# Layer norm rows applied one stage later, and each mixer's first products placed in the layer end before it

## The reference

```python
mod = cond @ ada_w[i] + ada_b[i]            # shift, scale, gate for two sites
h = x * (1 + scale[0]) + shift[0]
y = mixer_i(h)                              # 0 mlstm, 1 windowed attention, 2 hgrn2, 3 differential attention
x = layer_norm(ALPHA * x + (1 + gate[0]) * y, ln_g[i, 0], ln_b[i, 0])
h = x * (1 + scale[1]) + shift[1]
y = (silu(h @ w_gate) * (h @ w_up)) @ w_down
x = layer_norm(ALPHA * x + (1 + gate[1]) * y, ln_g[i, 1], ln_b[i, 1])
```

## Time and profile before

| | |
|---|---|
| time, median of 3 runs | 2500.95 us (2500.87 to 2510.68) |
| the profiled execution | 2511.77 us, of which the span is 2510.0 us |
| PE busy | 2339.4 us, 93% |
| DVE busy | 1841.5 us, 73% |
| ACT busy | 1165.9 us, 46% |
| POOL busy | 129.1 us, 5% |
| DMA | 575.95 MB, mean 229 GB/s |

### The profile page before, as it was taken

The page is one execution under the profiler, slowest core; times in us unless marked ns, Lnnn a source line. Parts: engine busy times, 40 slices in busy tenths (PEclk is TensorE's granted clock), DMA queues, the critical chain, the costliest instruction groups (busy, mean ns, idle before and its releaser), DMA issues. The chain is left out here.

```text
span 2510.0 us, 34924 instructions
## 1 busy us (share of the span) xinstructions
PE 2339.4 (93%) x14183; PEld 2064.0 (82%) x14183; DVE 1841.5 (73%) x2124; ACT 1165.9 (46%) x1260; POOL 129.1 (5%) x229
## 2 busy tenths in 40 slices
PE   7999988999999999899999988999997999998997
PEld 7888667788787888687998877898886998887996
DVE  6887676588888888666887637886585887676545
ACT  4342333477677777443443432443642443453442
POOL 1000100000000000001110000110001110000000
PEclk9999989899999999999999989999998999998999
DMA  8843642599999999566898225994534898334551
GB/s 302 255 136 101 198 151 68 161 360 366 357 365 360 358 366 354 198 215 212 268 371 293 93 101 162 369 345 124 167 107 145 281 369 290 97 126 148 187 186 68
DMA packets 414099, 575.95 MB, mean 229 GB/s; under 512 B 68848, under 2 KB 313072, under 8 KB 413936
## 3 DMA queue, kind: packets, MB, share of 16 engines
q1 hardware_dynamic: 393200, 498.17, 59.9%
q0 software_dynamic: 20736, 75.51, 8.0%
HBM read 572.54 MB, written 1.05 MB: 229 GB/s over the span
## 5 line engine op out<-in xcount | busy, mean ns | idle before, releaser
L286 DVE TENSOR_TENSOR st_lo<-st_raw,st_hi 128x2048 fp32r<-128x2048 f32 (+1 forms) x194 | 441.1, 2281 | 220.3 <-ACT st_hi L276 219.9
L276 ACT CAST st_hi<-st_raw 128x2048 fp32r<-128x2048 f32 (+1 forms) x194 | 367.4, 1899 | 358.9 <-PE ps L316 307.4
L314 PE MATMUL ps<-sb_h_hi,st_hi 128*128 128x256 f32 x1608 | 457.2, 284 | 15.5 <-DVE sb_h_lo L961 6.9
L315 PE MATMUL ps<-sb_h_lo,st_hi 128*128 128x256 f32 x1608 | 456.4, 284 | 0.0
L316 PE MATMUL ps<-sb_h_hi,st_lo 128*128 128x256 f32 x1608 | 456.3, 284 | 0.0
L286 DVE TENSOR_TENSOR es_lo<-es_raw,es_hi 128x2048 fp32r<-128x2048 f32 x192 | 428.1, 2285 | 1.1 <-ACT es_hi L276 0.8
L276 ACT CAST es_hi<-es_raw 128x2048 fp32r<-128x2048 f32 x192 | 367.6, 1915 | 85.7 <-PE ps L316 61.8
L314 PEld LDWEIGHTS ps<-sb_h_hi,st_hi 128*128 128x128 f32 x1608 | 309.0, 192 | 19.4 <-issue 10.1
L315 PEld LDWEIGHTS ps<-sb_h_lo,st_hi 128*128 128x128 f32 x1608 | 309.2, 192 | 1.6
L316 PEld LDWEIGHTS ps<-sb_h_hi,st_lo 128*128 128x128 f32 x1608 | 309.2, 192 | 0.2
L314 PE MATMUL ps<-st_hi,sb_h_hi 128*128 128x256 f32 (+1 forms) x528 | 186.2, 353 | 28.0 <-DVE st_lo L286 22.4
(11 more groups left out here) (680 smaller groups left out, 4211.0 us busy)
## 6 DMA issues: line engine op xcount, KB each, us to landing
st_raw<-in_ffn_w_in_dram SPq DMA_DIRECT2D x88, 1024.0 KB, 7.4
t_aw<-in_ada_w_dram POOLq DMA_DIRECT2D x144, 512.0 KB, 7.1
es_raw<-in_w_expert_gate_dram SPq DMA_DIRECT2D x128, 512.0 KB, 6.5
es_raw<-in_w_expert_up_dram SPq DMA_DIRECT2D x128, 512.0 KB, 8.1
es_raw<-in_w_expert_down_dram SPq DMA_DIRECT2D x64, 1024.0 KB, 7.3
st_raw<-in_ffn_w_out_dram SPq DMA_DIRECT2D x44, 1024.0 KB, 7.0
fb_aw<-in_ada_w_dram SPq DMA_DIRECT2D x39, 512.0 KB, 6.1
hs_raw<-in_w_in_dram SPq DMA_DIRECT2D x36, 512.0 KB, 7.9
```

The source lines that it names most:

```text
L276: act.copy(p.at(self.hi[:, m % self.held, :]), p.at(self.raw[:, n % self.slots, :])).then_inc(self.high, 1)
L286: dve.tensor_tensor(p.at(self.lo[:, m % self.held, :]), p.at(self.raw[:, n % self.slots, :]), p.at(self.hi[:, m % self.held, :]).bitcast(F ...
L314: pe.matmul(out, a_hi, b_hi, start=start, stop=False, skip_group_check=True)
L315: pe.matmul(out, a_hi, b_lo, start=False, stop=False, skip_group_check=True)
```

## The change

1. **Old rows in the mixer.** A class `PastNorm` loads the two rows of layer `i - 1`'s last norm at the start of mixer `i` (for mixers 1 to 3), and DVE applies them there: at marks 16 and 26 in the windowed and the differential mixer, after pieces 2 and 3 of the first projection in `hgrn`. The tail neither loads nor applies them. It also loads only the two `lnr` rows that it uses (four in the last layer).
2. **First products in the layer end.** At the end of tails 0 to 2 the 13 dummy matmuls go, and PE does the first piece of the next mixer (48 matmuls of 256 columns) as the splits come: `open_tokens` ahead of the windowed and differential mixer, `open_features` ahead of `hgrn`. ACT and DVE also lift and lower the next mixer's second piece in the layer end. The mixer skips what is taken.
3. **Finer first splits.** `divide` goes in five steps (blocks 0, 1, 2-3, 4-5, 6-7), at both sites; one transposed block moves to another PSUM bank.
4. **Initial stage.** DVE lowers the first weight piece ahead of its splits of the normed input; PE does that piece (24 matmuls) in this stage; ACT and DVE lift and lower two more there.
5. **Last norm.** For the last layer each token block is done by two fused instructions for each half (subtract the mean and multiply by gain; multiply by the spread's root and add the bias), the first block before the second one's adds.

```diff
@@ layer_tail, SP
+            S.send(sp, f0 + 2)
+            lines = [A["ln_g_2"][layer, 0], A["ln_b_2"][layer, 0]]
+            if final:
+                lines += [A["ln_g_2"][layer, 1], A["ln_b_2"][layer, 1]]
-            if layer:
-                for r, v in enumerate((A["ln_g_2"][layer - 1, 1], A["ln_b_2"][layer - 1, 1])):
-                    sp.dma_start(past[:, r, :], rows(v)).then_inc(past_landed, 16)
...
-            S.send(sp, S.reach(f_end, min(f_end + 1, len(S.pieces))))
+            S.send(sp, S.reach(f_end, min(f_end + 2, len(S.pieces))))
@@ layer_tail, PE
                 turn_norm(1, 1)
-                stir(k, pe, 0, 13)
+                ready = lambda kt: (hs, len(SPLITS) + splits_for(kt))
+                (open_features if layer == 1 else open_tokens)(k, pe, ready)
@@ layer_tail, ACT
             if not final:
+                S.lift(act, f_end + 2)
                 act.wait_ge(merged, 1)
                 modulated(1)
@@ layer_tail, DVE
-            if layer:
-                scale_past(0)
             S.lower(dve, o + 4)
-            if layer:
-                scale_past(1)
...
+            def centre_row(t):
+                for c in range(2):
+                    cols = slice(c * BANK, (c + 1) * BANK)
+                    dve.scalar_tensor_tensor(X[:, t, cols], X[:, t, cols], mv[:, 1, t, 0:1], lnr[:, 2, cols],
+                                             ALU.subtract, ALU.mult).then_inc(centred, 1)
...
             if not final:
+                normalise(1, 1)
                 divide(1)
+                S.lower(dve, f_end + 2)
@@ new
+class PastNorm:
+    def load(self, sp):
+        for r, name in enumerate(("ln_g_2", "ln_b_2")):
+            sp.dma_start(self.rows[:, r, :], rows(self.A[name][self.layer - 1, 1])).then_inc(self.landed, 16)
+    def scale(self, dve, t):
+        x = self.k.X[:, t, :]
+        dve.wait_ge(self.landed, 32)
+        dve.tensor_tensor(x, x, self.rows[:, 0, :], ALU.mult).then_inc(self.step, 1)
+        dve.wait_ge(self.step, t + 1)
+        dve.tensor_tensor(x, x, self.rows[:, 1, :], ALU.add).then_inc(self.done, 1)
+
+def open_tokens(k, pe, ready):
+    S = k.stream
+    wh, wl = S.take(pe)
+    for kt in range(8):
+        pe.wait_ge(*ready(kt))
+        for t in range(2):
+            last = product(pe, k.ps[:, 0, t * HB:(t + 1) * HB], k.h_hi[:, kt, t * P:(t + 1) * P],
+                           k.h_lo[:, kt, t * P:(t + 1) * P], wh[:, kt, :], wl[:, kt, :], kt == t == 0, kt == 7)
+    last.then_inc(S.used, 1)
@@ windowed, DVE
-            weave(w.dve_chunks(dve), masks_in(dve), w.dve_ropes(dve, cos, sin), w.dve_biases(dve), w.dve_mixes(dve),
-                  w.dve_stores(dve))
+            weave(w.dve_chunks(dve), masks_in(dve), w.dve_ropes(dve, cos, sin), past.scaling(dve, (16, 26)),
+                  w.dve_biases(dve), w.dve_mixes(dve), w.dve_stores(dve))
```

117 lines of the change are left out of this document (79 added, 38 removed).

## The result

The changed kernel took 2478.58 us (median of 10 runs, 2468.70 to 2505.52), the kernel before 2505.40 us (10 runs, 2500.32 to 2512.06): 0.9904 of it, 95% interval 0.9875 to 0.9934. That is faster, as forecast, but by 26.8 us and not by 40.3, and outside the range of 2450 to 2475. The two profiled executions hide this: 2510.0 us of span before, 2469.0 after, a difference of 41.0 us.

The account below looks back on a forecast made before the run. TensorE, busy almost everywhere, was taken to be bound by waits for VectorE's lower halves of weight pieces and at layer boundaries. 28.3 + 3.7 + 2.0 + 1.5 + 2.5 + 3.3 - 1.0 = 40.3 us off 2500.95 gave 2460.7, range 2450 to 2475.

Parts of the forecast that it names:

- Step 1: Tails of layers 1 to 3: moving the old norm's rows out gains 28.3 us, lower bound 22.4.
- Step 2: Mixers 1 to 3: applying the old rows on VectorE there costs 1 us in all, bounds 0 and 5.
- Step 3: Layer ends 0 to 2: early first products gain 3.7 us ahead of `hgrn`, 2.0 windowed, 1.5 differential.
- the new boundary is 2.1 us later than the old: Layer ends: lowering the second piece there delays the next mixer's start by 2.1 us; the 48 products finish under it.
- the clock rival: Layer ends and woven mixers: 48 products at low clock lose 3.5 us per end, new waits 1.5; 2474 us, chance 14%.
- 3.7 us gained: Layer 1's end into `hgrn`: 5.8 us of warm products leave the mixer, less 2.1 for the later boundary.
- TensorE waits 2.7 us: Start of the windowed mixer: new TensorE wait for the first rotation, leaving a gain of 2.0 us, bounds 0.5 and 5.
- three small instructions more in the same place: Differential mixer's start: no copies but three small instructions more at the first rotation; gain 1.5 us, bounds 0.5 and 5.
- Step 4: Finer first splits, first site: gain 0, at most 0.7 us in each of four layers; wait after G0 about 1 us.
- Step 5: Initial stage: TensorE's first product comes earlier, near 14.2 us; gain 2.5 us, bounds 0 and 3.5.
- Step 6: Last norm: fused instructions shorten the program's end; gain 3.3 us, bounds 2.5 and 3.6.
- Late rows: Rival, two mixers: rows land 14.3 us after issue, delaying VectorE and the rotation, 6.4 us each; 2473.5 us, chance 8%.

Follow-up runs that it names:

- the version with early rotations: Changed kernel with the first rotation ahead of the second piece in both woven mixers and the lambda work a chunk later: 2472.35 us (0.9872).
- the five without openings: Profiles without first products in the layer ends: two of the kernel before, two with only the old rows moved, one of the kernel without openings; means 104.7, 179.8, 133.1 us.
- the kernel without openings: Changed kernel with the layer ends' dummy matmuls back and no piece of the next mixer taken or split ahead: 2480.40 us (0.9891).
- the last experiment: Changed kernel with first rotation first, lambda work and old rows later, and one differential-mixer lowering behind the first factors, second old-row pair ahead of it: 2464.32 us (0.9834).
- the version without the rows: Changed kernel with first rotation ahead of the second piece and lambda work behind the second rotation, old norm's rows neither loaded nor applied: 2461.44 us (0.9821).

## Why the forecast was wrong, step by step

**Step 1, old rows out of the tails (28.3).** Right. With the rows moved alone the three stretches fell by 11.2, 11.2 and 5.7 us against the mean of before, 28.1 in all; forecast 11.6, 11.2 and 5.5. What I left out is the feed-forward part of layer 1, 4.2 us more, with the piece that landed late there before.

**Step 2, old rows in the mixers (1, bounds 0 and 5).** Within its bounds, but for another reason than given. I looked for the cost in the woven mixers; there the rows cost nothing in the changed kernel, because TensorE waits ahead of them anyway, and 3.4 to 4.1 in the differential mixer once that wait is removed. In `hgrn` they cost TensorE 1 to 2 us, at the wait that the forecast did not have.

**Step 3, first products in the layer end (7.2). This is the step that failed.** By its own terms:
- "the new boundary is 2.1 us later than the old": 2.6 where the clock held, up to 3.4 in layer 2, 4.6 to 5.2 in layer 1. I took the last lowering as what ends the layer (it ends 8.2 us behind the transposes). Where the clock held, SyncE's issue behind that lowering ends it, 0.5 us later than I counted. Elsewhere the 48 products do: they end at up to 11.4 us, since they begin behind waits of 2.00 and about 1 us and the clock had fallen. This is the clock rival, to which I gave 14%; its low clock came at two of three ends, with a boundary 1 to 3 us later instead of 3.5.
- "3.7 us gained" ahead of `hgrn`: 0.6 by the stretches, which is within chance. I had no new wait there ("none in `hgrn`"). TensorE waits 2.1 to 2.8 us for a lower half instead of 0.9, and 4.2 to 4.4 where the layer end kept its clock: it cannot pass that piece earlier, whenever the first products are done. The piece hangs on ScalarE's gates, they on VectorE's copy, and that on the queue with the old rows.
- "TensorE waits 2.7 us": 2.89 in the windowed mixer, right.
- "three small instructions more in the same place", 1.5 us gained in the differential mixer: 4.1 lost. VectorE stood 1.03 us on two small rows from the DMA for them, ScalarE's drain stood behind their Exp, TensorE waited 4.69 (up to 5.9 in four profiles) and then ran at 0.58. I had priced the instructions and not what they wait for. Moved away alone they gave nothing (137.0), and with the first rotation in front 0.7 (136.2): the lowering, the small rows and the old rows each hold the queue when the one before is gone, and the stretch falls to 133.2 and 129.1 only as the last of them move or go.

Together -0.3 + 0.6 - 4.1 = -3.8 instead of +7.2: 11 us of the 40 forecast. Ahead of the windowed mixer the boundary (2.6) and the rotation (2.9) take back what 48 warm products (5.8) bring.

**Step 4 (0).** Right; the wait behind G0 grew from 0.30 to 0.73, forecast about 1. **Step 5 (2.5).** 102.5 - 99.1 = 3.4. **Step 6 (3.3).** 18.0 - 14.6 = 3.4. **Late rows.** They landed in 7.8 us and held VectorE for 0.6 to 1.1: false in the changed kernel, true for the version with early rotations. That the measured difference, 26.8 us, is the clock rival's sum to the tenth is chance: it has 10.5 us in late boundaries alone, where the profile has some 4.

**The base.** I subtracted from 2500.95, the median of three runs. The median of 81 is 2506.0. The steps came from a profile of 2510.0, at a clock of 0.961, and its difference to the profile of after contains the clock of both. As measured by stretches the steps sum to 28.1 + 4.2 - 3.8 + 3.4 + 3.4 = 35.3 us; the medians over all runs differ by 24.6. The profiles lie between. Those of the changed kernel have a mean span of 2474.3 us, those of before 2505.2: 30.9 apart. Two of the four have a long low stretch of some 10 us that the sum leaves out, 5 us on the mean, and that brings 35.3 to 30.3. The other 6.3 are in the choice of executions: the four that were profiled took 2476.1 us on average, 5.3 under the median of the 27, and the two of before 1.0 over theirs. With only the rows moved the profiles (25.9) and the medians (2506.0 - 2480.5 = 25.5) agree, though the stretches named above sum to 32.3 there too; the difference lies in stages that the change does not touch, 4 us of it in one profile's hybrid block.

What makes the long low stretches stays open. Of the 15 profiles of kernels with openings four have one of 9 to 13 us at the end of a feed-forward part (one of them two), and two lost some 10 us ahead of the experts. Of the five without openings none has the first kind, and one lost 4 us ahead of the experts. That fits in its sign, but five are few, the experts come before the first opening of a layer end, the kernel without openings has no better median, and at an equal mean clock the two kernels lie 22.7 us apart.

## What to carry to other kernels

When work is moved ahead of a boundary, the gain is only paid if every engine's queue behind the boundary moves too: here each remedy showed the next instruction in VectorE's queue (lowering, small rows, old rows, factors). With the queues moved the first products do pay. Against the five profiles without openings the last experiment gained 104.7 - 102.2 = 2.5 and 133.1 - 131.3 = 1.8 us in the woven mixers, and the version without the rows 2.6 and 4.0, where the forecast had 2.0 and 1.5. Price a queued instruction by what it waits for, not by its length. And where executions of one kernel differ by 37 us, take differences stage by stage from more than one profile of each, and the base from many runs.

## What the hardware showed that I had not expected

- One program on one core runs at a mean granted clock between 0.956 and 0.969 from one execution to the next, and its time goes with it: 2505.52 us at 0.956, 2470.37 at 0.969. The step from the 2.4 to the 1.2 GHz level often begins behind a wait of 0.9 to 2.0 us, and the same wait may leave the clock at 1.00. The Trainium skill ("TensorE: Matmul & The Clock Gate", Part 1) says that the monitor runs free of the kernel and that one kernel measures different numbers of cold matmuls. The runs agree with the second: the end of layer 1 had its 48 products at 0.66 to 0.73 in the changed kernel's profiles and at 1.00 in two of other versions, behind the same 2.0 us wait (1.1 in one of the former).
- A fall can last: 24 us at 0.50 to 0.54, the lower of its two levels, with TensorE busy all the time.
- A 512 KB broadcast took 14.3 us from issue to landing behind other loads (kernel before) and 7.8 us with fewer beside it (changed kernel).
